# First stage of a two-block transformer kernel: halves of the first norm, a later place for the angles, and gate input products on both sides of two projection tiles

## The reference

```python
x = layer_norm(x, ln_in_g, ln_in_b)          # first norm
for i in range(2):
    h = x @ w_in[i]                          # input projection, 1024 -> 1704
    q, k, v, indexer parts = split(h)        # rotated by cos and sin of positions * inv
    ...                                      # two kinds of attention, w_o, norm
    ple = (p[i] @ w_pp[i]) * sigmoid(x @ w_pg[i])   # "gate input": p @ w_pp
    ...                                      # gated feed-forward, norm
```

## Time and profile before

| | |
|---|---|
| median of 3 runs | 1554.91 us (1549.75 to 1555.19) |
| span of the profiled execution, first to last instruction | 1552.6 us |
| the profiled execution's own time | not recorded apart from its span |
| TensorE busy | 1497.1 us, 96% |
| VectorE busy | 1062.8 us, 68% |
| ScalarE busy | 778.0 us, 50% |
| GpSimd busy | 123.2 us, 8% |
| mean granted TensorE clock | 0.990 of full |

### The profile page before, as it was taken

One profiled execution on the slowest core, in us unless ns is written; L12 is line 12 of the kernel. 1 busy time (PEld: TensorE's weight loads), 2 busy tenths in 40 slices (PEclk: granted clock), 3 DMA queues, 4 the chain that ended last, 5 costly groups with the idle time before them and its releaser, 6 DMA issues.

```text
span 1552.6 us, 21682 instructions
## 1 busy us (share of the span) xinstructions
PE 1497.1 (96%) x8433; PEld 1264.8 (81%) x8433; DVE 1062.8 (68%) x1713; ACT 778.0 (50%) x1162; POOL 123.2 (8%) x98
## 2 busy tenths in 40 slices
PE   8999999999899999999999999999999999999997
PEld 5877888888677888878877988888788779888886
DVE  7777587667766787676345566878863555677777
ACT  4563544444554444434565344666545653446563
POOL 0130000000210000011022000000010320000000
PEclk9999999999999999999999999999999999999999
DMA  7534655656235655644614745556536147345551
GB/s 260 196 101 138 217 190 190 212 172 209 93 119 172 235 190 190 226 157 135 193 56 152 252 134 172 185 190 216 176 121 195 54 151 257 126 168 184 189 190 66
DMA packets 184429, 265.03 MB, mean 171 GB/s; under 512 B 7368, under 2 KB 139398, under 8 KB 184200
## 3 DMA queue, kind: packets, MB, share of 16 engines
q1 hardware_dynamic: 178712, 258.38, 50.2%
q10 hardware_dynamic: 5616, 5.26, 1.0%
HBM read 258.38 MB, written 5.24 MB: 170 GB/s over the span
## 4 chain that ended last, share of the span: by engine, by line
PE 77%; DVE 13%; ACT 4%; issue 3%; DVEq 2%; POOL 1%; ACTq 0%; POOLq 0%; DMA 0%; SPq 0%
PE psw L815 18%; PE psw L814 8%; PE psw L742 8%; PE psw L744 7%; PE psw L743 7%; DVE wlo L1735 5%; PE psa L742 4%; PE psa L744 4%; PE psa L743 4%; PE psa L876 3%; PE psa L874 3%; PE psa L926 2%; PE psw L898 2%; PE psa L943 1%; PE psw L818 1%
## 5 line engine op out<-in xcount | busy, mean ns | idle before, releaser
L1735 DVE TENSOR_TENSOR wlo<-raw,whi 128x2048 fp32r<-128x2048 f32 (+3 forms) x199 | 449.9, 2266 | 124.5 <-ACT whi L1347 124.1
L815 PE MATMUL psw<-xboth,whi 128*128 128x512 f32 x1344 | 464.7, 396 | 1.2 <-DVE wlo L1735 1.2
L1347 ACT ACTIVATE whi<-raw 128x2048 fp32r<-128x2048 f32 (+3 forms) x199 | 375.0, 1885 | 175.6 <-PE psw L744 91.3
L814 PE MATMUL psw<-xboth,wlo 128*128 128x256 f32 x1176 | 327.9, 279 | 0.0
L815 PEld LDWEIGHTS psw<-xboth,whi 128*128 128x128 f32 x1344 | 242.7, 188 | 49.1 <-DVE wlo L1735 2.3
L814 PEld LDWEIGHTS psw<-xboth,wlo 128*128 128x128 f32 x1176 | 221.7, 189 | 7.5
L742 PE MATMUL psw<-whi,xboth 128*128 128x512 f32 (+3 forms) x472 | 181.8, 385 | 6.4 <-DVE wlo L1735 5.3
L744 PE MATMUL psw<-whi,xboth 128*128 128x512 f32 (+3 forms) x472 | 178.8, 379 | 0.0
L743 PE MATMUL psw<-wlo,xboth 128*128 128x512 f32 (+3 forms) x472 | 178.6, 378 | 0.0
L1409 ACT ACTIVATE r<-psw 128x512 f32<-128x512 f32 x88 | 52.5, 596 | 174.7 <-PE psw L815 164.2
L742 PE MATMUL psa<-whi,rr 128*128 128x512 f32 x352 | 137.5, 391 | 1.4 <-DVE rr L2365 1.3
(11 more groups left out here) (290 smaller groups left out, 2209.9 us busy)
## 6 DMA issues: line engine op xcount, KB each, us to landing
raw<-in_w_gu SPq DMA_DIRECT2D x44, 1024.0 KB, 5.1
raw<-in_ffn_w_up SPq DMA_DIRECT2D x42, 1024.0 KB, 5.1
raw<-in_w_down SPq DMA_DIRECT2D x22, 1024.0 KB, 4.9
raw<-in_ffn_w_down SPq DMA_DIRECT2D x22, 1024.0 KB, 4.8
raw<-in_w_in SPq DMA_DIRECT2D x20, 1024.0 KB, 5.3
raw<-in_xa_wkv SPq DMA_DIRECT2D x16, 1024.0 KB, 5.4
raw<-in_w_o SPq DMA_DIRECT2D x8, 1024.0 KB, 5.2
raw<-in_w_out SPq DMA_DIRECT2D x8, 1024.0 KB, 5.2
```

The costliest lines, as they stand in the source:

```text
L814: pe.matmul(bank[:, 0:S], wl[:, k, cols], xhi[:, k, :], start=False, stop=False)
L815: ins = pe.matmul(bank.rearrange("p (i s) -> p i s", i=2), wh[:, k, cols], xboth[:, :, k, :], start=k == 0, stop=k == KD - 1)
L1347: nc.scalar.activation(tile_flat("hi", i), tile_flat("raw", i), ACT.Copy).then_inc(hi_ready, 1)
L1735: v.tensor_tensor(tile_flat("lo", i), tile_flat("raw", i), tile_flat("hi", i).bitcast(F32), ALU.subtract).then_inc(lo_ready, 1)
```

## The change

Three edits, all in the first stage. (1) The first norm waits for its spread rows in three steps: the gain halves ahead of the first pass, then each bias half ahead of its half of the second pass. (2) `angles()` moves on VectorE from behind the first norm to behind `turned_lo` of token tile 1, and `tables()` behind the statistics of the memory; on ScalarE the sine moves behind `turned_hi` of token tile 1. (3) On TensorE the gate input products of token tile 1 move, in layer 0, behind tiles 1 and 2 of the projection, and on ScalarE the split of tile 3 is called ahead of the two copies of token tile 1. In layer 1 the order is as before.

```diff
@@ TensorE
-                for t in range(NT):
-                    if t and l:
-                        norm_turns(x_in, 0)
+                def gate_input(t):
                     for half in range(2):
                         for kk in range(2):
...
                         ins.then_inc(tile_done if t and half else pp_part, 1)
+
+                def second_in_turns():
+                    if l == 0:
+                        gate_input(1)
+                    norm_turns(x_in, 1)
+                gate_input(0)
+                if l:
+                    norm_turns(x_in, 0)
+                    gate_input(1)
...
-                            {(2, 0): lambda: norm_turns(x_in, 1), (3, 0): param_turns,
+                            {(2, 0): second_in_turns, (3, 0): param_turns,
@@ ScalarE
             split(1)
-            act.wait_ge(angles_ready, 1)
-            nc.scalar.activation(angs[:, 4:6, :], angs[:, 4:6, :], ACT.Sin).then_inc(sines_ready, 1)
...
                     if t == 0 and l == 0:
                         split(2)
                         nxt[0] = 2
+                        serve((1, "pp", l, 0))
                     elif t == 0:
                         turned_hi(x_in, 0)
                 serve((1, "pp", l, 0))
 
                 def second_tokens():
                     turned_hi(x_in, 1)
+                    if l == 0:
+                        act.wait_ge(angles_ready, 1)
+                        nc.scalar.activation(angs[:, 4:6, :], angs[:, 4:6, :], ACT.Sin).then_inc(sines_ready, 1)
@@ VectorE
                 if t == 0 and nm["n"] == 0:
-                    dve.wait_ge(gb_ready, 2 * NT)
+                    dve.wait_ge(gb_ready, NT)
...
                     h = slice(half * 512, (half + 1) * 512)
+                    if t == 0 and nm["n"] == 0:
+                        dve.wait_ge(gb_ready, NT + half + 1)
...
             norm((1, "in", 0), xtok, 0)
-            angles()
             turned_lo((1, "in", 0), 0)
...
                     turned_lo((1, "in", 0), 1)
-                    tables()
+                    angles()
                     dve.wait_ge(mem_loaded, 16 * NT)
                     for t in range(NT):
                         half_stats(memory, t)
+                    tables()
```

## The result

The changed kernel took 1561.02 us (median of 6 runs, 1559.94 to 1562.85), the one before in the same session 1554.49 us (6 runs, 1549.52 to 1555.19). The ratio is 1.005, its 95% interval 1.0035 to 1.0064: slower, by about as much as half a per cent. The profiled execution spans 1558.9 us, 6.3 more than before, and took 1560.98 us.

What follows compares the result with a forecast made beforehand. TensorE bounds the kernel, busy 1497.1 of 1552.6 us. Waits of 1.8 + 2.6 = 4.4 us plus 0.6 for the clock make 5.0, against the 1554.9 us median giving 1560 us; range 1554 to 1564.

Steps and rivals of the forecast that it cites:

- The head start: First norm by halves: TensorE turns token tile 0 1.8 us earlier; first four gate products end at 17.4, 2.2 earlier.
- Tile 2 loses its cover: Input projection: without the second four gate products ahead, TensorE waits 1.9 us for weight tile 2's low part.
- The gate products behind tile 2 and the count that tile 3 waits for: Tile 3's split waits for the moved gate products; TensorE waits some 3.2 us, tile 3 starts 1.8 us later.
- The angles: Moved on VectorE to a place without gaps, 3.7 us of work delays tile 4's low part; TensorE waits 2.6 us.
- The sum of the waits: First stage: 1.8 us at tile 3 plus 2.6 at tile 4, together 4.4 us; bounds 3.4 and 5.7.
- The clock term: TensorE's clock falls behind an unswallowed wait, costing 1.0 us; 0.6 us added for an even chance behind tile 4's wait.
- The shift carried to the end: Behind tile 4 TensorE's work keeps its old order, VectorE gets none added; the shift stays to the end.
- A: Rival: clock falls behind each wait, not swallowed; slower by over 0.5%, 7.7 to 8.7 us, about 1563 us; chance 0.10.
- B: Rival: head start survives, tile 3's split not hanging on the gate products; 1553 to 1557 us; chance 0.11.
- C: Rival: angles stay hidden in a VectorE gap, costing less than 2.6 us; 1556 to 1558 us; chance 0.07.

Runs made afterwards that it cites:

- the two later profiles: The changed kernel run again twice, unaltered, beside the kernel before: 1561.06 us (ratio 1.0046) and 1560.38 us (ratio 1.0040).
- room for tile 3: Changed kernel, but the high part of weight tile 3 no longer waits for a finished tile: 1559.21 us, ratio 1.0036 to the kernel before.
- third time: The changed kernel, unaltered, measured a third time, beside the kernel with filled waits: 1560.38 us, ratio 1.0040 to the kernel before.
- early high parts: Kernel before with first edit, tile 2's high part ahead of ScalarE's gate input copies, tile 3's split not waiting for a finished tile: 1551.71 us, ratio 0.9978.
- the kernel with the angles back: Changed kernel with the second edit taken back, angles and sine at their old place: 1558.34 us, ratio 1.0036 to the kernel before.

## Why the prediction was right

I said 1560 us; it was 1561.0, within the range, and on the border of half a per cent.

*The head start* was real: the transposes of token tile 0 ended at 12.59 (forecast 12.95), the first four gate products at 16.8 (forecast 17.4, bounds 16.4 to 18.7; 17.6 in the two later profiles). The level of the clock in that stretch is read from the length of the records: the clock column shows 1.00 there throughout, though one record takes 0.89 and a later one 0.43 us. The first edit alone shows it kept to the end of the stage, 2.7 us.

*Tile 2 loses its cover*: forecast a wait of 1.9 us, measured 1.62, 1.85 and 1.84 in the three profiles of the changed kernel.

*The gate products behind tile 2 and the count that tile 3 waits for*: forecast a wait of 3.2 us and tile 3 at 31.4, measured 3.52 and 31.33. That the place fits to 0.1 us is luck: the gate products ended 0.6 us early, and from there to tile 3 it took 14.6 us, not 13.9, since tile 2 took 2.4 instead of 2.2 us and each hand-over to the next engine a little. The kernel with room for tile 3 shows that the count was the cause. The third edit alone loses against the kernel before.

*The angles*: forecast 2.6 us of wait for tile 4. The first two edits together gave 2.60. In the changed kernel the low part of tile 4 was there at 44.7, against 44.8 forecast; the wait read 1.15 only because TensorE itself came later, with the slower clock behind tile 3. The forecast said that such a fall would be swallowed by the wait for tile 4, and in all three profiles it was, to 0.1 us. (VectorE was not quite without a gap at the new place of the angles: it waits 0.6 us for GpSimd's power in both kernels, which changes nothing in the sum.)

*The sum of the waits* was forecast at 4.4 us, and the first profile has 44.71 - 40.40 = 4.3 us at tile 4, 4.5 at the index scores.

*The clock term* is the mis-sized one. I priced a fall at 1.0 us, from memory products of which only a part lay in the slow stretch, and added 0.6 for an even chance (half of 1.0 would be 0.5). The fall behind the wait of the two-edit kernel took 1.85 us, those behind the wait for tile 2 1.5 us. In two of three profiles of the changed kernel such a fall and a later rise of the clock in the first gate products brought the index scores to 66.14, 6.9 us late and not 4.5. In the sum I had allowed for an unswallowed fall only behind the wait for tile 4, where the changed kernel showed none (1.00 from 40 to 50 us in all three profiles); it came behind the wait for tile 2. The Trainium skill ("TensorE: Matmul & The Clock Gate", part 1) says that the moment at which the clock changes varies from run to run. The trace agrees for the rise: the first four gate products, in which it lies, took 4.39, 5.16 and 5.17 us in three executions of one program. At tile 2 a wait of 1.62 us had no fall behind it and waits of 1.85 and 1.84 had one; whether the moment or the 0.2 us decided, no run here separates. That by the rule a wait of 2.6 us brings a fall in some runs only was my own reading; one profile has a fall behind such a wait, and no run shows how often.

*The shift carried to the end.* I carried the 4.4 us unchanged past tile 4. The stage's shift did grow once more, by 1.7, 1.6 and 1.5 us in the three profiles, at the memory products, because the fall that the kernel before hides there came behind a wait instead. That term was not in the sum, so that 1560 came so near to 1561 owes something to luck: the 0.6 us that I added for the clock stand for effects that were larger and at other places. This reading comes from the rows; no kernel was run that moves this fall alone.

*The rivals.* A (falls that are not swallowed) had one half of its condition right: a fall reached the products of tile 2 in two of three profiles, more often than its 0.10 says. The other half, a fall behind tile 4, did not come, and the total stayed under its own 1563 us. B (the head start survives) fell to the wait list; it needed both the count and the angles out of the way. C (angles hidden) fell to the wait of 2.60.

*What stays open.* The spans of single executions differ by more than this stage does: the profile of the third time is 1557.8 us with the index scores at 66.14, the first is 1558.9 with 63.70. The rows show where that comes from. The third is 8.5 us behind the kernel before until the products L876, at 776.93 against 768.44, and 5.2 behind at the next ones, at 788.40 against 783.21: there the profile of the kernel before has a slow stretch (0.76 from 770 to 780 us), and the third has none (1.00 from 770 to 800). So part of each difference in span is where the one profile of the kernel before happened to have its falls. How often each fall comes in the executions that were not profiled, and so how the 6.5 us in the median divide, is not settled; the waits of 4.3 us are.

## What to carry to other kernels

Before moving work that seems to stand in the way, ask what it covers: here the gate products were the cover of one weight split and the release of another, and moving them opened a wait of 1.6 us and one of 3.5. A load or a split that waits for a count of finished tiles moves with whatever raises the count. An idle wait on TensorE costs more than its length where the clock falls behind it and no later wait swallows the slow stretch.

## What the runs showed of the hardware that I had not expected

A wait as short as 1.84 us, in a stretch of otherwise dense products, had a fall of the clock behind it (third time, 20 to 30 us at 0.83 of full), while the waits of 1.10 us in the kernel before and of 1.39 us with early high parts had none, and useless products in the same waits kept the clock at 1.00. The length of a wait alone does not decide: before the memory products a wait of 3.05 us had a fall behind it (5.41 us for sixteen) and one of 3.03 us, in the kernel with the angles back, had none (3.72 us). A fall took 1.4 to 2.6 us of TensorE's time in this stage, and it cost the kernel that time only where no later wait swallowed it.
